# Relative-position bias from a host-laid table and one copy less, and unheld projection loads, in a two-layer encoder kernel

## What is computed

```
proj = rmsnorm(x) @ w_in                  # 1024 x 3072, six column blocks of 512
# four differential-attention heads ("A"), 256 x 256 scores:
s = q @ k.T + t5_bias[t5_bucket(kpos - qpos)]
# eight 2-D neighbourhood heads ("B"), grid of 4 rows x 64 columns, window of 16 columns:
s = q @ k.T + rpb[head, key_row - query_row + 7, key_col - query_col + 15]
mix = concat(heads) @ w_out
```

## Time and profile before

| what | value |
|---|---|
| median of 3 runs | 1304.08 us (1303.95 to 1305.77) |
| the profiled execution's own time | 1304.42 us |
| its span (first to last instruction) | 1302.2 us |
| PE, DVE, ACT, POOL busy | 79%, 22%, 10%, 3% of the span |
| mean GB/s of all transfers | 343 |
| q1, SP's queue of weights | 438.32 MB |
| q0, POOL's queue | 7.36 MB |
| q10, ACT's queue | 0.53 MB |

### The profile page before, as it was taken

How to read it: one execution, slowest core, us unless ns; L and a number is a source line. 1 busy time by engine, 2 the same in 40 slices (tenths; PEclk the granted TensorE clock), 3 DMA queues, 4 the chain that set the end, 5 groups by cost and what they waited for, 6 DMA issues and landing times.

```text
span 1302.2 us, 12358 instructions
## 1 busy us (share of the span) xinstructions
PE 1030.4 (79%) x5102; PEld 456.5 (35%) x5102; DVE 281.5 (22%) x613; ACT 132.0 (10%) x282; POOL 41.3 (3%) x54
## 2 busy tenths in 40 slices
PE   6689999866885868777969899988758676777686
PEld 5456654312321323123347444623213232232132
DVE  2044434101210211011232343432102110121013
ACT  1012410000000000000113011100000000000001
POOL 2530000100000000000000000000000000000000
PEclk9899999878888898788979999998879888887798
DMA  7893375999999999999953314689999999999993
GB/s 241 224 363 135 119 324 234 410 429 426 428 428 428 429 428 428 428 427 427 392 207 129 129 65 182 270 340 427 428 427 429 428 428 429 428 429 426 430 419 127
DMA packets 51428, 446.91 MB, mean 343 GB/s; under 512 B 5350, under 2 KB 7470, under 8 KB 27312
## 3 DMA queue, kind: packets, MB, share of 16 engines
q1 hardware_dynamic: 47504, 438.32, 81.6%
q0 software_dynamic: 3584, 7.36, 2.2%
q10 hardware_dynamic: 288, 0.53, 0.1%
HBM read 445.10 MB, written 3.97 MB: 345 GB/s over the span
## 4 chain that ended last, share of the span: by engine, by line
DMA 54%; PE 40%; DVE 3%; issue 2%; SPq 1%; ACT 1%; DVEq 0%; POOL 0%
DMA sb_weights<-moe_w_up 49%; PE psum L1298 38%; DMA sb_weights<-ev_w_in 2%; DMA rpb_rows<-rpb_scratch 1%; SPq L465 1%; DMA sb_x<-x 1%; PE psum L1308 0%; PE psum L1409 0%; DMA t_scratch<-sb_weights 0%; PE psum L1317 0%; ACT sb_hn L588 0%; PE psum L1456 0%; DVE sb_weights L812 0%; DVE sb_small L814 0%; DVE sb_weights L776 0%
## 5 line engine op out<-in xcount | busy, mean ns | idle before, releaser
L1298 PE MATMUL psum<-sb_weights,sb_hT 128*32 128x512 f32 (+2 forms) x2368 | 528.2, 695 | 215.2 <-DMA sb_weights<-moe_w_up 107.7
L1298 PEld LDWEIGHTS psum<-sb_weights,sb_hT 128*32 128x32 f32 (+2 forms) x2368 | 158.6, 138 | 573.7 <-issue 369.7
L1298 PE MATMUL psum<-sb_weights 128*32 128x512 f32 (+9 forms) x1514 | 295.3, 550 | 13.9 <-DMA sb_weights<-moe_w_down 7.3
L1298 PEld LDWEIGHTS psum<-sb_weights 128*32 128x32 f32 (+6 forms) x1514 | 106.9, 135 | 176.1 <-issue 163.4
L1207 DVE TENSOR_TENSOR sb_weights<-sb_weights,psum 96x512 f32<-96x512 f32 (+1 forms) x22 | 15.0, 684 | 551.1 <-PE psum L1298 551.1
L1298 PE MATMUL psum<-sb_hT,sb_weights 128*128 128x256 f32 (+1 forms) x400 | 93.0, 393 | 2.6 <-DMA sb_weights<-ev_w_in 1.8
L1298 PEld LDWEIGHTS psum<-sb_hT,sb_weights 128*128 128x128 f32 (+1 forms) x400 | 76.1, 193 | 19.6 <-issue 5.9
L1220 DVE TENSOR_TENSOR sb_x<-sb_x,psum 128x512 f32<-128x512 f32 x88 | 60.5, 688 | 27.5 <-PE psum L1298 27.5
L1298 PEld LDWEIGHTS psum<-sb_weights,sb_hn 128*128 128x128 f32 x384 | 60.0, 190 | 5.7 <-issue 5.3
L1298 PE MATMUL psum<-sb_weights,sb_hn 128*128 128x192 f32 (+1 forms) x384 | 61.1, 317 | 0.0
L691 ACT ACTIVATE sb_weights<-psum 96x512 f32<-96x512 f32 (+1 forms) x22 | 13.0, 593 | 344.0 <-PE psum L1298 344.0
(11 more groups left out here) (190 smaller groups left out, 382.3 us busy)
## 6 DMA issues: line engine op xcount, KB each, us to landing
sb_weights<-moe_w_gate SPq DMA_DIRECT2D x64, 2048.0 KB, 29.0
sb_weights<-moe_w_up SPq DMA_DIRECT2D x64, 2048.0 KB, 27.8
sb_weights<-moe_w_down SPq DMA_DIRECT2D x60, 2048.0 KB, 27.9
sb_weights<-od_w_in SPq DMA_DIRECT2D x6, 2048.0 KB, 19.9
sb_weights<-ev_w_in SPq DMA_DIRECT2D x5, 2048.0 KB, 32.2
sb_weights<-moe_w_down SPq DMA_DIRECT2D x8, 1024.0 KB, 15.9
sb_weights<-ev_w_out SPq DMA_DIRECT2D x2, 2048.0 KB, 27.9
sb_weights<-od_w_out SPq DMA_DIRECT2D x2, 2048.0 KB, 8.1
```

Of the source, the lines that this page charges most:

```text
L1298: return nc.tensor.matmul(o, l, r, start=start, stop=stop, skip_group_check=True)
```

## The change

`repeated_rows` builds the B heads' rows on the host, each repeated 64 times and with -1e30 around the table, as a new input `rpb_rows` (2 halves x 8 heads x 6 shifts x 64 x 128 floats). POOL reads `biasB` from it in two transfers, one for each 64 partitions. `biasB` keeps six key-row shifts for a half (3072 values a partition); VectorE takes four of them, from an offset that depends on the tile. The A heads' `t5_rows` is written straight from the four SBUF partitions of `t5rel`. The product that fills `t5rel` is moved ahead of the wait for the last `hT_done`, and its copy goes from VectorE to ScalarE. lambda gets a tile of its own. SP no longer waits ahead of unit 2, nor at its start.

```
+SHIFTS = 2 * (ROWS - 1)
...
+def repeated_rows(rpb):
+    lo = NA_MAX_ROWS - ROWS
+    rows = np.full((P // GRID_W, B_HEADS, SHIFTS, P), MASKED, np.float32)
+    mid = GRID_W - NA_COLS
+    for half in range(P // GRID_W):
+        first = lo + 1 - half
+        rows[half, :, :, mid:mid + 2 * NA_COLS - 1] = np.asarray(rpb)[0, :, first:first + SHIFTS, :]
+    rows = rows.reshape(-1, 1, P)
+    return np.ascontiguousarray(np.broadcast_to(rows, (rows.shape[0], GRID_W, P)))
...
@@ SP
                 for c in range(IN_UNITS):
-                    if layer == 0 and c == 2:
-                        sp.wait_ge(rows_written, 32)
...
-            sp.wait_ge(gp_done, 2)
             for layer in range(2):
@@ POOL
-            gp.memset(rpbx, MASKED).then_inc(gp_done, 1)
...
-            gp.wait_ge(gp_done, 2)
-            gp.dma_start(rpbx[0:B_HEADS * NDR, mid:mid + 2 * NA_COLS - 1],
-                         A["ev_rpb"][0, :, lo:lo + NDR, :]).then_inc(rpb_loaded, 16)
...
-            gp.wait_ge(rpb_loaded, 16)
-            gp.dma_start(rpb_dram, rpbx[0:B_HEADS * NDR, :]).then_inc(scratch_written, 16)
             gp.wait_ge(t5_done, 1)
-            gp.dma_start(t5_dram, t5rel[0:A_HEADS, :]).then_inc(scratch_written, 16)
-            gp.wait_ge(scratch_written, 32)
-            gp.dma_start(t5_rows, t5_dram.unsqueeze(1).to_broadcast([A_HEADS, P, 2 * SEQ])
+            gp.dma_start(t5_rows, t5rel[0:A_HEADS, :].unsqueeze(1).to_broadcast([A_HEADS, P, 2 * SEQ])
                          ).then_inc(rows_written, 16)
-            gp.dma_start(rpb_rows, rpb_dram.unsqueeze(1).to_broadcast([B_HEADS * NDR, GRID_W, P])
-                         ).then_inc(rows_written, 16)
-            gp.wait_ge(rows_written, 32)
+            rpb = A["rpb_rows"]
+            for half in range(P // GRID_W):
+                src = bass.AP(rpb.tensor, half * B_HEADS * SHIFTS * GRID_W * P + GRID_W - 1,
+                              [[P - 1, GRID_W], [GRID_W * P, B_HEADS * SHIFTS], [1, GRID_W]])
+                dst = biasB[half * GRID_W:(half + 1) * GRID_W].rearrange("p h (m c) -> p (h m) c", c=GRID_W)
+                gp.dma_start(dst, src).then_inc(biasB_loaded, 16)
+            gp.wait_ge(rows_written, 16)
             for t in range(TILES):
                 gp.dma_start(biasA[:, t], ...
-            for t in range(TILES):
-                for rr in range(P // GRID_W):
...
-                        gp.dma_start(biasB[rr * GRID_W:(rr + 1) * GRID_W, t, :, i * GRID_W:(i + 1) * GRID_W],
-                                     src).then_inc(biasB_loaded, 16)
...
@@ ACT, mixer0
+                act.wait_ge(t5_psum, 1)
+                nc.scalar.activation(t5rel[0:A_HEADS, :], psum[0:A_HEADS, 7], ACT.Copy).then_inc(t5_done, 1)
                 act.wait_ge(lam_sum, 1)
@@ DVE, mixer0
-                dve.wait_ge(t5_psum, 1)
-                nc.vector.tensor_copy(t5rel[0:A_HEADS, :], psum[0:A_HEADS, 7]).then_inc(t5_done, 1)
...
-                prod = rpbx.rearrange("p (a d) -> p a d", a=2)
-                dve.wait_ge(scratch_written, 32)
+                prod = lamprod.rearrange("p (a d) -> p a d", a=2)
...
-                        bias = biasB[:, t, 2 * i:2 * i + 2, :]
+                        at = (ROWS - 2 - t * (P // GRID_W)) * GRID_W
+                        bias = biasB[:, 2 * i:2 * i + 2, at:at + SEQ]
@@ PE
                 for t in range(TILES):
                     turn_h(layer, t)
+                if layer == 0:
+                    pe.wait_ge(t5_loaded, 32)
+                    mm(psum[0:A_HEADS, 7], t5w[0:T5_BUCKETS, :], t5in[0:T5_BUCKETS, :], True, True
+                       ).then_inc(t5_psum, 1)
                 pe.wait_ge(hT_done, 4 * (2 * layer) + 4)
```

More of the change, by code:

```diff
@@ L183, in build @@
         biasA = carve(TILES * A_HEADS * SEQ).rearrange("p (t h k) -> p t h k", t=TILES, h=A_HEADS)
-        biasB = carve(TILES * B_HEADS * SEQ).rearrange("p (t h k) -> p t h k", t=TILES, h=B_HEADS)
+        biasB = carve(B_HEADS * SHIFTS * GRID_W).rearrange("p (h k) -> p h k", h=B_HEADS)
         sc = carve(2 * HALF).rearrange("p (b n) -> p b n", b=2)
@@ L194, in build @@
         t5rel = carve(2 * SEQ)
-        rpbx = carve(P)
+        lamprod = carve(2 * A_DH)
         used[0] = 0
@@ L250, in build @@
         y = hn
-        t5_dram = nc.dram_tensor("t5_scratch", (A_HEADS, 2 * SEQ), F32, kind="Internal").ap()
-        NDR = 2 * ROWS - 1
-        rpb_dram = nc.dram_tensor("rpb_scratch", (B_HEADS * NDR, P), F32, kind="Internal").ap()
         t5_rows = nc.dram_tensor("t5_rows", (A_HEADS, P, 2 * SEQ), F32, kind="Internal").ap()
-        rpb_rows = nc.dram_tensor("rpb_rows", (B_HEADS * NDR, GRID_W, P), F32, kind="Internal").ap()
         in_full = [sem(f"in_full{c}") for c in range(IN_UNITS)]
@@ L272, in build @@
         wr_scaled = sem("wr_scaled")
-        rpb_loaded = sem("rpb_loaded")
-        scratch_written = sem("scratch_written")
         rows_written = sem("rows_written")
@@ L508, in _ @@
             gp.dma_start(t5w[0:T5_BUCKETS, :], A["t5_bias"]).then_inc(t5_loaded, 16)
-            gp.wait_ge(gp_done, 2)
-            mid = GRID_W - 1 - (NA_COLS - 1)
-            lo = NA_MAX_ROWS - ROWS
-            gp.dma_start(rpbx[0:B_HEADS * NDR, mid:mid + 2 * NA_COLS - 1],
-                         A["ev_rpb"][0, :, lo:lo + NDR, :]).then_inc(rpb_loaded, 16)
             gp.dma_start(lamrow, A["ev_lambda"].rearrange("l a d -> l (a d)").partition_broadcast(P)
@@ L553, in _ @@
             gp.wait_ge(cst_loaded, 16)
-            gp.wait_ge(biasB_loaded, 16 * (SEQ // GRID_W * ROWS))
-            b4 = biasB.rearrange("p t h (i c) -> p (t h i) c", c=GRID_W)
-            gp.tensor_tensor(b4, b4, window.unsqueeze(1).to_broadcast([P, TILES * B_HEADS * ROWS, GRID_W]),
+            gp.wait_ge(biasB_loaded, 16 * (P // GRID_W))
+            b4 = biasB.rearrange("p h (m c) -> p (h m) c", c=GRID_W)
+            gp.tensor_tensor(b4, b4, window.unsqueeze(1).to_broadcast([P, B_HEADS * SHIFTS, GRID_W]),
                              ALU.add).then_inc(biasB_done, 1)
@@ L1438, in unit_step @@
                         turn(u - 1)
-                pe.wait_ge(t5_loaded, 32)
-                mm(psum[0:A_HEADS, 7], t5w[0:T5_BUCKETS, :], t5in[0:T5_BUCKETS, :], True, True
-                   ).then_inc(t5_psum, 1)
                 for g in range(6):
@@ L1725, in _ @@
                         all_rounds(more, past + it)
-_INS = ["x", "t5_bias", "norm_mix", "norm_ffn", "norm_final", "ev_w_in", "ev_lambda", "ev_subln", "ev_rpb", "ev_w_out",
+_INS = ["x", "t5_bias", "norm_mix", "norm_ffn", "norm_final", "ev_w_in", "ev_lambda", "ev_subln", "ev_w_out",
         "od_w_in", "od_w_gk_fwd", "od_b_gk_fwd", "od_w_gk_bwd", "od_b_gk_bwd", "od_out_norm", "od_w_out",
@@ L1742 @@
     arrays["moe_b_router"] = _np.concatenate([inputs["moe_b_grp"], inputs["moe_b_exp"]], axis=1)
+    arrays["rpb_rows"] = repeated_rows(inputs["ev_rpb"])
     arrays["cst"], arrays["t5_onehot"] = shape_constants()
```

## The result

The changed kernel takes 1311.74 us (median of 4 runs, 1310.61 to 1312.93) against 1304.09 us for the kernel before beside it (1303.95 to 1305.77). The ratio is 1.0054, with a 95% interval of 1.0039 to 1.0069: slower by half a percent, 7.65 us. The profiled execution has a span of 1309.7 us against 1302.2.

What follows compares the result with a forecast made beforehand. Over half the span ends on a transfer, mostly experts' weights; only the start of g = 6, layer 0's seventh projection group, matters. It moves from 73.79 to 78.0, +4.2 us: 1308 against the median of 1304.08; range 1287 to 1314.

Steps and rivals of the forecast that it cites:

- The frame: Layer 0's mixer: whatever it gains or loses moves everything behind it, from 216.88 us on, by as much.
- The copy's price: t5_rows from four SBUF partitions: 43.3 us at one engine's 26.8 GB/s, between 13.6 and 78 us.
- Rival A: At t5_rows: source doesn't matter, TensorE never stops, g = 6 at 58.6, gain 15.2, 1289 us; chance 0.34.
- the forecast's second support for it: Last 4 us of rpb_rows, queued behind t5_rows: 10.4% of 16, under two engines, agreeing with a copy on four engines.
- One packet from each queue in turn: DMA engines with work on both queues alternate one packet each, however long the other's lasts; 739 to 746 packets before.
- Rival B: At t5_rows: copy slow but engines not held; units 2 and 3 in time, A bias isn't; 1301.5 us; chance 0.13.
- C: Rival at t5_rows: four partitions give 13.4 GB/s, copy ends near 98, unit 2 40 us late, some 1343; chance 0.05.
- Which unit is late: Weights before g = 4: unit 2 lands at some 61.9, 6 us later than before; unit 3 by 77.
- unit 3 is there before g = 5 ends, so g = 6 starts at 78.0: Projections: unit 3 landed by 77, g = 5 ends at 78.0, so g = 6 starts then instead of 73.79.
- The clock: TensorE after its wait for unit 2: 0.52 of full clock in first 4.6 us, g = 4 and 5 take 16.15 us again.
- Nothing on the path: POOL waits, fewer issues, B copies, mask addition (8.84 us less a quarter), lambda's tile and removed waits cost TensorE nothing.

Runs made afterwards that it cites:

- e3: Kernel before with only SP's wait ahead of unit 2 taken away, both row copies still from HBM scratches: 1296.82 us, ratio 0.9944.
- e1: Kernel after with the A heads' rows stored to a scratch in HBM first and copied 128 times from there: 1295.74 us, ratio 0.9934.
- e4: Kernel after with the four source rows in partitions 0, 4, 8 and 12 instead of 0 to 3: 1289.43 us, ratio 0.9879.
- e2: Kernel after with SP's wait for the written rows ahead of unit 2 put back: 1330.29 us, ratio 1.0194.
- e5: Kernel after with the row copy cut into four transfers of one partition each, over up to 16 engines: 1312.68 us, ratio 1.0060.
- e9: Kernel of e1 with POOL's mask addition moved ahead of its small loads: 1288.55 us, ratio 0.9866.
- e10: Kernel after with HBM scratch, row copy over 128 partitions, A bias ahead of B bias, mask addition ahead of small loads: 1287.97 us, ratio 0.9863.
- e7: Kernel after with POOL's wait for the rows and the A bias ahead of the B bias: 1307.57 us (1302.51 to 1312.81), ratio 1.0015.

## Why the prediction was right, point by point

The forecast was 1308 us and slower; 1311.7 was measured. The cause it named, the copy's source, is the right one. That the number comes so near is in part luck, as the fourth and fifth points say.

- **The frame holds.** All that the mixer loses or wins arrives at the end. The marker (before, after, e3, e1, e4: 149.1, 157.0, 141.9, 141.4, 135.7) and the times (1304.1, 1311.7, 1296.8, 1295.7, 1289.4) move together within some 2 us. Taken from the profiled executions, e2, e5, e9 and e10 do too. e7 doesn't quite: its marker is 3.4 us later than before (152.46) and its profiled execution only 0.4 us longer (1304.85 against 1304.42). Along the chain of waits it is still 4.4 us behind the kernel before among layer 0's experts (464.12 against 459.73) and 0.7 near the end of the kernel (1279.62 against 1278.91). So those 3 us come back in between; why is open.
- **The copy's price.** Between bounds of 13.6 and 78 us I took one engine's worth of bandwidth, 43.3 us. It took 47.2 beside the weights and 44.9 alone. This was the choice on which the sign hung, made from no direct row; e4 and e2 showed it. Rival A is what happens when the source stops mattering: 1289, and e4 gives 1289.43. The nearest measured pace, 25 GB/s in e2, is a little under the 26.8 taken. That the copy lies on four engines is borne out by e2 (3.9 of 16); the forecast's second support for it, under two engines at work in the earlier trace rows, didn't show as much.
- **One packet from each queue in turn.** 16 to 16, 32 to 39 and 407 to 400 packets where both queues had work. Rival B, with engines that aren't held, falls; so does C, whose 13.4 GB/s are half of what was measured. C's own sum was also off: a copy that ends near 98 puts unit 2 at some 101, g = 6 at 117, and the time at 1347, not 1343.
- **Which unit is late.** Here the working was off twice, in opposite directions. I let the copy's long packets begin at 19.3. POOL's queue moves nothing from 20 to 21 us, and its first packets come after 21. From 22 to 26 us it moves 575 packets (below), most of them small: 562 of the stretch's 1154 packets are under 512 bytes. Its 0.11 MB has room for some 26 packets of 4 KB, 6.5 in a us, and that is the pace of the stretch from 40 to 45 us (32 in 5 us). So the copy is under way from some 21.5 us, 2 us later than I had it. In those 2 us the weights ran at full speed: SP's queue moves 194 packets from 20 to 21 us, 12 an engine. Every one of them that is through before the copy begins saves a slow turn, and unit 2 lands at 52.7 instead of 61.9. But the copy, begun later and a little slower, ended at 63.8 instead of 59.6, and the B bias behind it shared its turns with unit 3, which landed at 80.5 instead of 77. The step "unit 3 is there before g = 5 ends, so g = 6 starts at 78.0" failed: g = 5 ended at 68.8, and a second stop took its place. 9 us too late in one step and 11.7 us left out in the next nearly cancel; that is luck.

```profile
q1 hardware_dynamic: 579, 1.16, 76.9%
q0 software_dynamic: 575, 0.11, 30.9%
```

- **The clock.** The forecast had one stop. After the second, g = 6's first 16 matmuls take 5.51 us where before they took 3.72. The stretches (busy us of each engine, PEclk, DMA share, GB/s):

```profile
52.70:57.30 4.60, 4.56 (x6) 2.04 (x7) 0.00 (x0) 0.00 (x0) 0.00 (x0) 0.55 0.24 32
...
80.50:82.30 1.80, 1.78 (x4) 1.51 (x5) 0.00 (x0) 0.00 (x0) 0.00 (x0) 0.50 0.28 70
```

TensorE had stood idle for 7.43 and 11.74 us, and the granted clock is about half of full (the 1.2 GHz level of 2.4) just after. So the sum is 6.7 us (g = 6) plus 1.8 (clock), less 0.6 that VectorE's wait for POOL (the next point) is shorter than before: 7.9, the marker's move. I had 4.2, only the first term, and too small because of the second stop.
- **"Nothing on the path".** Right for the change itself by luck of timing. The mask addition does meet VectorE, which the sum left out: 0.9 us before, 0.3 after, but 4.6 to 5.0 in e1, e3 and e7. That term was missing from rival A too; e4, where it costs 0.8, shows A's time, and e1 and e3, where it costs 4.6 and 4.8 and slows the matmuls behind it, lie some 7 us above it.

## What to carry to other kernels

Before a transfer that reads few partitions many times, ask how many separate paths its source partitions use, and how many engines it takes: 1 MB from four neighbouring partitions took 45 us, from four partitions four apart 20, from HBM with 128 as outer dimension 9. A slow transfer costs more than its own wait, because each engine gives another queue one packet for each slow one, so all loads that need these engines drip. And when a hold on a queue is taken away, look for what it kept apart: alone it was a gain of 8 us here, together with the new source a loss of 8.

## What the runs showed that I had not expected

- A VectorE operation of one column with both inputs in SBUF ends with the POOL operation that was running on SBUF when it came, however long that takes. In all six kernels in which they meet (before, after, e1, e3, e4, e7), it ends 0.02 to 0.03 us after POOL's. VectorE's row is shown as busy, not as waiting, so the list of waits doesn't have it. The timeline of the kernel before (POOL's row is in the earlier trace rows) and of the kernel after (POOL's row stands in the section on the result):

```profile
82.63 1.07 DVE L823 TENSOR_TENSOR sb_small<-sb_small 128x1 f32<-128x1 f32 x1
```

```profile
91.15 0.46 DVE L814 TENSOR_TENSOR sb_small<-sb_small 128x1 f32<-128x1 f32 x1
```

74.83 + 8.84 = 83.67 and 82.63 + 1.07 = 83.70; 84.92 + 6.67 = 91.59 and 91.15 + 0.46 = 91.61. The bias additions, with one input in PSUM, run at 0.69 us beside POOL (86.81 in the kernel after). The Trainium skill has this in *SBUF — State Buffer*, "Who interferes with whom": such an operation contends with a GpSimd instruction that reads SBUF, and the second to come is fully blocked. All six cases agree.
- SP is held up in issuing. Issuing unit 4 took SP 27 us, from 17.0 to 44.1, and from 40 to 45 us all queues together kept under 5 of the 16 engines busy (23.8% and 5.8%), although units 4 and 5 were due next. Transfers of ev_w_in whose issue overlaps 30 to 50 us (shortest, median and longest issue in ns, then first and last start):

```profile
L416 SPq DMA_DIRECT2D sb_weights<-ev_w_in x2: 13413/20246/27078, 17.0 to 44.1; - x2
```

So four slow engines seem to hold back twelve fast ones; that SP waited for room in its queue is my reading, no run shows it. TensorE had no wait for units 4 and 5 in this kernel.
- Spreading a slow source over all engines (e5) isn't neutral: from 40 to 45 us every one of the 16 was occupied with it, at 30 GB/s in all.
